# The Pool mixing of a two-layer decoder step in three rounded passes, with a ring of six weight places

## The chip, the cores and the metric

The kernel runs on one core of a Trainium2 chip. It is written for the engines by hand: TensorE (PE, with its weight loads as PEld), VectorE (DVE), ScalarE (ACT), GpSimd (POOL) and SyncE (SP), which issues the DMAs. The metric is the device time of one execution in microseconds (us), the median of several runs.

## What is computed

The reference is one inference step of a decoder with two layers, for a prompt of 1024 tokens and 32 sample tokens (8 x 4), together T = 1056 columns. Layer 0 mixes tokens by multi-scale pooling:

```
zp = rms_norm(x) @ w_in_pool        # u (1536) | gate (1536) | memory query (512) | memory gate (512)
for g, w in enumerate((2, 4, 8, 16)):                     # four groups of 384 channels
    means = trailing mean of u over w positions
pooled = means - u
mixed = einsum('btgc,gcd->btgd', pooled, w_grp)           # 384 x 384 for each group
branch = mixed * scale
y = [branch * silu(gate), memory_attention * silu(memory gate)] @ w_out
x = x + y
```

Layer 1 does stick-breaking attention in the place of the pooling; the change doesn't touch it. Everything is float32.

## The kernel before

**Stages.** The layers come one after the other. Layer 0 is `front_phase` (norms, keys and values of the memory tokens, the transposed tokens; up to 91 us), `pool_phase` (the projection, the pooling, the mixing; 91 to 512 us), `memory_attention_phase` (to 597 us) and `out_phase`. Between two phases stands a barrier of all engines.

**The projection.** `Quads` computes the projection in pairs of 128-column blocks, 16 pairs p in layer 0, each by Strassen's scheme in seven products, P1 to P7 (`self.seq` has their order: P5, P4 of the pair before, P1, P2, P6, P3, P7). A product is 24 matmuls on 264 columns, since each float32 product is made in three rounded passes: high weights by high tokens (L320), high weights by low tokens (L321), low weights by high tokens (L322). "fp32r" is the rounded kind of float32. GpSimd combines the weights (`combine`, L192 to L204), ScalarE rounds them (`round`, L226) and VectorE subtracts for the remainder (`remainder`, L233). The weights stand in a ring of `RING` = 8 places, and each engine prepares the weights `AHEAD` = 7 products ahead of the one in hand. ScalarE copies P1, P6, P4 and P5 out of their banks (`copy`), VectorE adds P2, P3 and P7 (`add`). In the first products the tokens too have to be split, by ScalarE (`token_high`, L274) and VectorE (`token_rest`, L279).

**The groups.** Pairs 0 to 3 give queries and memory gates; then each group of the pooling has three pairs (`first(n) = 4 + 3 * n` is its first): u, u; u, gate; gate, gate. Its pooling (`pool_part`, VectorE) is spread over the products behind, and its mixing (`group`) comes behind product P1 of the next group's first pair, for the last group behind the last product. `group` transposes the kept rows for the state outputs (L1278) and makes nine outputs, three row blocks m by three column parts u, each of three float32 matmuls on 352 columns (L1291; the trace has two records for each such matmul, 54 in all). The outputs alternate between two banks, and VectorE scales and gates each (L1234). When y is out, SyncE stores it (L1064, in three parts), and then loads the next group's state (L1050) and mixing weights (L1052). TensorE turns that state (`turn_state`, L1270) behind product P2 of the next group's first pair:

```
                for i, (p, x) in enumerate(q.seq):
                    q.product(pe, i)
                    for n in range(GROUPS):
                        if n and (p, x) == (first(n), "P1"):
                            group(n - 1)
                        if (p, x) == (first(n), "P2"):
                            turn_state(n)
                group(GROUPS - 1)
```

**The end of the stage.** SyncE loads the first three pages of the samples' memory keys into freed memory (L931), and behind the last product of the projection the queries (`memory.queries`, L938), their scales (L939) and the prompt's own keys (L935); then it finishes the last group. GpSimd pads the samples' queries (`memory.pad`, L943, L950). The next stage's SyncE first waits until the last group's stores have landed (`memory.tail`) and then loads pages 3 and 4 of the keys (a_more, L931), which TensorE turns (L1526) behind pages 0 to 2.

**The end of the front.** `front_phase` prepares the first six weights of the ring beside its own work. GpSimd's combination for P3 (L204) waits for the remainder of P2's weights, the third of the ring; GpSimd's three token sums of tile 6 (L248, L254, L256) stand behind it, and VectorE's `other_sums(7)` (L248 on) waits for those.

Of the kernel before, what the change touches and what calls it, by code (L numbers as in the profile page):

```python
# [88 lines left out]
RING, AHEAD = 8, 7  # L89


class Quads:
# [11 lines left out]
    def __init__(self, nc, k, c, i, src, columns):  # L104
        self.nc, self.k, self.i, self.src, self.columns, self.n = nc, k, i, src, columns, len(columns)
        self.full, self.lo = [], []
        for n in range(7):
            self.allocate_tokens(n)
        self.w_hi = k.sb("w_hi", [P, RING, K2, P], F32R)
        self.w_full, self.w_lo = self.two_kinds("w_lo", [P, RING, K2, P])  # L110
# [46 lines left out]

    def load_b(self, sp, p):
# [23 lines left out]
    def combine(self, gp, i):  # L182
# [5 lines left out]
        if x == "P5":  # L188
            if i >= RING:
                gp.wait_ge(self.done, 2 * (i - RING) + 2)  # L190
            gp.wait_ge(self.loaded_b[p % 2], 16 * (p // 2 + 1))
            gp.tensor_tensor(self.w_full[:, i % RING, :, :], a21, a22, ALU.add).then_inc(self.combined, 1)  # L192
# [13 lines left out]
    def source(self, i):  # L206
        p, x = self.seq[i]
        if x == "P5":
            return self.w_full[:, i % RING, :, :]
# [3 lines left out]
    def round(self, act, i):  # L213
# [4 lines left out]
        if i >= RING:  # L218
            act.wait_ge(self.done, 2 * (i - RING) + 2)
# [6 lines left out]
        act.activation(self.w_hi[:, i % RING, :, :], self.source(i), ACT.Copy).then_inc(self.high, 1)  # L226

    def remainder(self, dve, i):
# [4 lines left out]
        dve.tensor_tensor(self.w_lo[:, i % RING, :, :], self.source(i), self.w_hi[:, i % RING, :, :].bitcast(F32),  # L233
# [64 lines left out]
    def product(self, pe, i):  # L298
# [4 lines left out]
        for n in range(2):  # L303
# [13 lines left out]
            for kk in range(K2):  # L317
                w_hi, w_lo = self.w_hi[:, i % RING, kk, :], self.w_lo[:, i % RING, kk, :]
# [108 lines left out]
def front_phase(nc, c, A, O, S, q, source):  # L427

    with ExitStack() as ctx:
# [35 lines left out]
        with nc.Block() as block:  # L465
# [71 lines left out]
            def _(act):  # L537
# [123 lines left out]
                for j in range(3):  # L661
# [12 lines left out]
            def _(dve):  # L674
# [134 lines left out]
                for j in range(3):  # L809
# [3 lines left out]
                first_sum(7)  # L813
                other_sums(7)
# [85 lines left out]
class MemoryAhead:  # L900
# [11 lines left out]
    def __init__(self, nc, k, c, A, S, i):  # L912
        self.nc, self.c, self.A, self.S, self.i = nc, c, A, S, i
        self.at = nc.sbuf_top - self.BELOW[i] - self.SIZE
        self.kl = [k.sem(f"kl{n}") for n in range(self.PAGES[i])]
# [21 lines left out]
    def queries(self, sp):  # L937
        sp.dma_start(self.qT[:, :, :], self.S[f"mq{self.i}"].rearrange("h p t -> p h t")).then_inc(self.ql, 16)  # L938
        sp.dma_start(self.rs[:, :], self.S[f"rs{self.i}"]).then_inc(self.rl, 16)  # L939

    def pad(self, gp):
# [3 lines left out]
        gp.wait_ge(self.ql, 16)  # L945
# [63 lines left out]
def pool_phase(nc, c, A, O, S, q, memory):  # L1009

    with ExitStack() as ctx:
# [6 lines left out]
        wg = k.sb("wg", [P, GB, GW])  # L1018
        up = k.sb("up", [P, GB, HIST + T])
        us = k.sb("us", [P, GB, NB_S, SX])  # L1020
        sums = [k.sb(f"sum{i}", [P, EXT]) for i in range(2)]
# [7 lines left out]
        tail = k.sb("tail", [KEPT, GW])  # L1029
        q.allocate_banks(k)  # L1030
        aux = k.ps("aux", 2)
        names = "gated zeroed keeps stl sturned wgl mready mixed pooled sums tailt tailc stored ystored carried".split()
# [9 lines left out]
        with nc.Block() as block:  # L1042
            @block.sync
            def _(sp):
# [9 lines left out]
                def finish_group(n):  # L1054
# [3 lines left out]
                    sp.dma_start(O["pool_p"][0, 0, :, g * GW:(g + 1) * GW], tail[0:HIST, :]  # L1058
                                 ).then_inc(memory.tail if last else s["stored"], 16)
                    sp.dma_start(O["pool_s"][0, :, HIST - T_S:HIST, g * GW:(g + 1) * GW], tail[HIST:KEPT, :]  # L1060
                                 ).then_inc(memory.tail if last else s["stored"], 16)
# [4 lines left out]
                for j in range(AHEAD - 1):  # L1066
# [3 lines left out]
                for i, (p, x) in enumerate(q.seq):  # L1070
                    q.loads(sp, i + AHEAD - 1)
# [21 lines left out]
                memory.queries(sp)  # L1093
# [9 lines left out]
            def _(gp):  # L1103
# [11 lines left out]
                for j in range(6, AHEAD + 1):  # L1115
                    q.combine(gp, j)
                for i, (p, x) in enumerate(q.seq):
                    q.combine(gp, i + AHEAD + 1)
# [16 lines left out]
            def _(act):  # L1135
                def begin(p):
# [13 lines left out]
                    q.copy(act, p, "P5", part(p, 1, 1), ACT.Copy)  # L1150
                q.tokens_scalar(act, 0)
                for j in range(6, AHEAD):
                    q.round(act, j)
                for i, (p, x) in enumerate(q.seq):
                    q.round(act, i + AHEAD)
# [1979 lines left out]
```

## Time and profile before

| | us |
|---|---|
| median of 3 runs | 2334.16 |
| lowest and highest | 2331.37, 2334.32 |
| profiled execution | 2338.4 |
| its span in the trace | 2336.7 |
| TensorE busy | 2201.2 |
| VectorE busy | 1292.6 |
| ScalarE busy | 1009.2 |
| GpSimd busy | 433.0 |

Times in the trace count from the span's start. A busy time is the union of an engine's instructions, and matmuls are pipelined, so that a busy TensorE is not one at its peak; the distance from one start to the next is what a matmul takes of a run. An idle time in square brackets is what the engine stood before an instruction, with what ended it.

### The profile page before, as it was taken

What the parts mean: (1) busy time and instruction counts of PE and PEld (TensorE: products, weight loads), DVE (VectorE), ACT (ScalarE), POOL (GpSimd) and SP (SyncE); (2) the same over time, 40 slices, a digit from 0 to 9 for tenths busy, and PEclk for the clock granted to TensorE, in tenths of its full rate; (3) what the DMA queues carried; (4) which work ended last, traced back from release to release, by engine and by line L of the source; (5) the groups of instructions that cost most, each with busy time, mean ns of one, the idle gap of its engine ahead of it and who ended that gap; (6) DMA issues with size and microseconds to landing.
All of it is one profiled execution on the core that took longest, in us unless ns stands there. A gap on an engine that the chain in (4) does not pass through costs nothing. (4 is left out here: it accounts for less than half of the span.)

```text
span 2336.7 us, 47103 instructions
## 1 busy us (share of the span) xinstructions
PE 2201.2 (94%) x18709; PEld 1834.6 (79%) x18709; DVE 1292.6 (55%) x2040; ACT 1009.2 (43%) x2090; POOL 433.0 (19%) x542
## 2 busy tenths in 40 slices
PE   7799999997999689999999998889999999998999
PEld 6799899886688589999999997766666566654787
DVE  6846666435422374334444443588888888875211
ACT  7533223215311144333333343457777777775100
POOL 0533223202000043222222221321121111100000
PEclk9899999998899889999999999889999999999999
DMA  8222222144635553334433336789999999978331
GB/s 289 86 87 89 79 64 66 66 166 163 210 119 155 146 186 102 109 99 133 153 106 109 96 96 234 253 292 379 396 407 393 406 395 388 375 284 307 123 108 55
DMA packets 283274, 453.98 MB, mean 194 GB/s; under 512 B 30962, under 2 KB 208062, under 8 KB 283038
## 3 DMA queue, kind: packets, MB, share of 16 engines
q1 hardware_dynamic: 274958, 421.83, 51.8%
q0 software_dynamic: 8000, 29.10, 3.3%
q8 instruction: 149, 2.44, 0.4%
q14 instruction: 71, 0.58, 0.1%
q10 hardware_dynamic: 96, 0.02, 0.0%
HBM read 372.43 MB, written 78.43 MB: 193 GB/s over the span
## 5 line engine op out<-in xcount | busy, mean ns | idle before, releaser
L233 DVE TENSOR_TENSOR h_w_lo<-l_w,h_w_hi 128x512 fp32r<-128x512 f32 x264 | 213.7, 811 | 221.2 <-ACT h_w_hi L226 218.7
L226 ACT ACTIVATE h_w_hi<-l_w 128x512 fp32r<-128x512 f32 x264 | 166.7, 633 | 239.9 <-PE i_c L322 81.4
L320 PE MATMUL i_x<-h_t_hi,h_w_hi 128*128 128x264 f32 x560 | 163.3, 292 | 6.8 <-DVE h_t_lo L279 6.8
L2960 PEld LDWEIGHTS b_krow<-ar_arena,b_qd 128*32 128x32 f32 x3072 | 107.2, 111 | 72.6 <-issue 57.0
L192 POOL TENSOR_TENSOR h_w_lo_full<-l_w 128x512 f32<-128x512 f32 x44 | 57.5, 1308 | 560.5 <-DMA l_w<-in_w_in_sb_dram 229.9
L320 PE MATMUL i_y<-h_t_hi,h_w_hi 128*128 128x264 f32 x560 | 161.3, 288 | 0.0
L322 PE MATMUL i_x<-h_t_hi,h_w_lo 128*128 128x264 f32 x560 | 161.0, 287 | 0.0
L321 PE MATMUL i_x<-h_t_lo,h_w_hi 128*128 128x264 f32 x560 | 160.4, 286 | 0.0
L321 PE MATMUL i_y<-h_t_lo,h_w_hi 128*128 128x264 f32 x560 | 159.0, 284 | 0.0
L322 PE MATMUL i_y<-h_t_hi,h_w_lo 128*128 128x264 f32 x560 | 158.9, 284 | 0.0
L2960 PE MATMUL b_krow<-ar_arena,b_qd 128*32 128x128 f32 x3072 | 140.7, 279 | 7.9 <-ACT b_kev L2666 6.9
L320 PE MATMUL i_c<-h_t_hi,h_w_hi 128*128 128x264 f32 x448 | 129.4, 289 | 17.8 <-DVE h_t_lo L279 17.4
L2789 DVE STREAM_TRANSPOSE ar_arena<-ar_arena 128x768 f32<-128x768 f32 x146 | 140.7, 967 | 1.3 <-PE b_krow L2960 1.3
L2907 PE MATMUL b_zbank<-bf_qh,bf_kh 128*128 128x512 f32 (+3 forms) x288 | 133.7, 548 | 2.2 <-PEq L76 2.2
L321 PE MATMUL i_c<-h_t_lo,h_w_hi 128*128 128x264 f32 x448 | 128.4, 287 | 0.0
L322 PE MATMUL i_c<-h_t_hi,h_w_lo 128*128 128x264 f32 x448 | 128.1, 286 | 0.0
L2647 ACT ACTIVATE b_a<-b_a 128x512 f32<-128x512 f32 (+2 forms) x144 | 75.2, 522 | 104.1 <-DVE b_a L2749 103.4
L2923 PE MATMUL b_obank<-b_a,b_vh 128*128 128x512 f32 (+3 forms) x288 | 117.9, 491 | 1.8 <-issue 0.8
L200 POOL TENSOR_TENSOR l_w<-l_w 128x512 f32<-128x512 f32 x44 | 65.3, 1485 | 282.1 <-DVE h_w_lo L233 282.1
L320 PEld LDWEIGHTS i_x<-h_t_hi,h_w_hi 128*128 128x128 f32 x560 | 107.0, 191 | 7.5 <-issue 7.4
L321 PEld LDWEIGHTS i_x<-h_t_lo,h_w_hi 128*128 128x128 f32 x560 | 107.2, 192 | 0.0
L322 PEld LDWEIGHTS i_x<-h_t_hi,h_w_lo 128*128 128x128 f32 x560 | 107.1, 191 | 0.0
(368 smaller groups left out, 6424.9 us busy)
## 6 DMA issues: line engine op xcount, KB each, us to landing
ar_arena<-in_cache_sb_k_dram SPq DMA_DIRECT2D x73, 768.0 KB, 9.7
bf_vpage<-in_cache_sb_v_dram SPq DMA_DIRECT2D x64, 768.0 KB, 8.8
b_vpage<-in_cache_sb_v_dram SPq DMA_DIRECT2D x64, 768.0 KB, 8.5
l_w<-in_w_in_sb_dram SPq DMA_DIRECT2D x56, 512.0 KB, 3.9
l_w<-in_cache_sb_k_dram SPq DMA_DIRECT2D x36, 768.0 KB, 9.4
l_w<-in_w_in_pool_dram SPq DMA_DIRECT2D x32, 512.0 KB, 4.2
bf_kpage<-in_cache_sb_k_dram SPq DMA_DIRECT2D x19, 768.0 KB
ar_arena<-scratch_yT SPq DMA_DIRECT2D x14, 1024.0 KB, 6.6
```

The source lines that it names most:

```text
L192: gp.tensor_tensor(self.w_full[:, i % RING, :, :], a21, a22, ALU.add).then_inc(self.combined, 1)
L200: gp.tensor_tensor(a11, a22, a21, ALU.subtract).then_inc(self.combined, 1)
L226: act.activation(self.w_hi[:, i % RING, :, :], self.source(i), ACT.Copy).then_inc(self.high, 1)
L233: dve.tensor_tensor(self.w_lo[:, i % RING, :, :], self.source(i), self.w_hi[:, i % RING, :, :].bitcast(F32), ALU.subtract).then_inc(self.r ...
L320: pe.matmul(out, w_hi, t_hi, start=kk == 0 and x in ("P1", "P2", "P5"), stop=False, skip_group_check=True)
L321: pe.matmul(out, w_hi, t_lo, start=False, stop=False, skip_group_check=True)
L322: ins = pe.matmul(out, w_lo, t_hi, start=False, stop=kk == K2 - 1, skip_group_check=True)
L2647: act.activation(a[:, t % 3, 0:n], a[:, t % 3, 0:n], ACT.Exp).then_inc(s["ax"], 1)
L2789: dve.transpose(kt[u % 2][:, :, :, x * Q:(x + 1) * Q].rearrange("p h f j -> p (h f) j"), kpage[n % NK][:, u % 2 * HH * HD:(u % 2 + 1) * HH ...
L2907: ins = pe.matmul(zbank[t % 2][:, 0:n], kh[:, h % 2, kb * P:(kb + 1) * P], qh[:, h % 2, q0:q0 + n], start=True, stop=not diag, skip_group_ ...
L2923: pe.matmul(obank[:, 512 - n:512], vh[:, h % 2, kb, :], a[:, t % 3, 0:n], start=first, stop=last, skip_group_check=True).then_inc(s["pvd"], 1)
L2960: ins = pe.matmul(krow[pair * CT:(pair + 1) * CT, 0:P], qd[:, i % 2, at:at + CT], kt[u % 2][:, h, f, :], start=odd == 0 and f == 0, stop=o ...
```

## The change

It does five things. (1) The mixing is computed in three rounded passes (`product3`) on split pooled rows (`up_hi` in the two pooling buffers, `up_lo` over `up`) and split weights (`wg_hi`, `wg_lo` over `wg`). ScalarE rounds the weights in `mix_weights` and the rows in `mix_high`, in three parts of 128 x 1056 elements over two buffers; VectorE subtracts in `mix_weights` and `mix_low`. (2) The outputs come column part by column part, so that all three stores of y wait for the last three outputs. (3) The mixing of a group comes behind P2 of the next pair instead of P1. (4) In layer 0 the ring has six places (`self.ring`) and a lead of five (`self.ahead`); the two places that come free hold `wg_hi` and the tail rows. In the front, weights 2 and 3 are rounded later and remainder 2 stands behind `first_sum(7)`. (5) Head 0 of the queries and the prompt's own keys are loaded behind the last output of the last mixing (`mready`), since their place is in use until then; heads 1 to 3 behind the last product as before.

```diff
@@ Quads.__init__
+        self.ring = PLACES if i else PLACES - 2
+        self.ahead = self.ring - 1
...
@@ front_phase, scalar
                 act.wait_ge(s["made"], 12)
-                for j in range(3):
+                for j in range(2):
                     q.round(act, j)
                 key_root(1)
                 evacuate(7)
-                q.round(act, 3)
                 act.wait_ge(s["made"], 14)
-                for j in range(4, 6):
+                for j in range(2, 6):
                     q.round(act, j)
@@ front_phase, vector
-                for j in range(3):
+                for j in range(2):
                     q.remainder(dve, j)
                 key_normed(1)
                 evacuate(7)
                 first_sum(7)
+                q.remainder(dve, 2)
                 other_sums(7)
@@ pool_phase, sync
                     for m in range(GB):
-                        sp.wait_ge(s["mixed"], 9 * n + 3 * m + 3)
+                        sp.wait_ge(s["mixed"], 9 * n + 7 + m)
                         sp.dma_start(S["yT0"][g * GB + m], gate[:, m, :])
...
                 sp.wait_ge(q.done, 2 * len(q.seq))
-                memory.queries(sp)
+                memory.queries(sp, 1, MH)
+                memory.scales(sp)
+                sp.wait_ge(s["mready"], 9 * GROUPS)
+                memory.queries(sp, 0, 1)
                 memory.own_keys(sp)
                 finish_group(GROUPS - 1)
@@ pool_phase, scalar
+                def mix_weights(n):
+                    act.wait_ge(s["wgl"], 16 * (n + 1))
+                    if n:
+                        act.wait_ge(s["mready"], 9 * n)
+                    for kk in range(GB):
+                        act.activation(wg_hi[kk], wg[:, kk, :], ACT.Copy).then_inc(s["wgh"], 1)
+
+                def mix_high(n):
+                    act.wait_ge(s["pooled"], GB * (n + 1))
+                    for u in range(NT):
+                        if u >= 2:
+                            act.wait_ge(s["mready"], 9 * n + 3 * (u - 1))
+                        act.activation(up_hi[u % 2], up[:, :, HIST + u * TT:HIST + (u + 1) * TT], ACT.Copy
+                                       ).then_inc(s["uph"], 1)
...
+                        for n in range(1, GROUPS):
+                            if p + 1 == first(n):
+                                mix_high(n - 1)
                         if p + 1 < q.n:
                             begin(p + 1)
...
+                mix_high(GROUPS - 1)
@@ pool_phase, vector
+                def mix_low(n, u):
+                    dve.wait_ge(s["uph"], NT * n + u + 1)
+                    cols = slice(HIST + u * TT, HIST + (u + 1) * TT)
+                    dve.tensor_tensor(up_lo[:, :, cols], up[:, :, cols], up_hi[u % 2].bitcast(F32), ALU.subtract
+                                      ).then_inc(s["upr"], 1)
+
                 def mix(n):
+                    mix_low(n, 0)
+                    mix_low(n, 1)
...
+                    for u in range(NT):
+                        if u == 1:
+                            mix_low(n, 2)
+                        for m in range(GB):
+                            dve.wait_ge(s["mready"], 9 * n + 3 * u + m + 1)
@@ pool_phase, tensor
-                    pe.wait_ge(s["wgl"], 16 * (n + 1))
-                    for m in range(GB):
-                        for u in range(NT):
-                            at = 3 * m + u
+                    pe.wait_ge(s["wgr"], GB * (n + 1))
+                    for u in range(NT):
+                        pe.wait_ge(s["upr"], NT * n + u + 1)
+                        for m in range(GB):
+                            at = 3 * u + m
...
-                        if n and (p, x) == (first(n), "P1"):
+                        if n and (p, x) == (first(n), "P2"):
                             group(n - 1)
                         if (p, x) == (first(n), "P2"):
                             turn_state(n)
```

TensorE, at the first group's mixing, before: behind the last pass of P1 (bank y) come the transposes of the kept rows, the 27 float32 matmuls, P2 (bank x, of its 24 passes the first and last are shown), and the turning of the state.

```order
L322 MATMUL p_y<-h_t_hi,h_w_lo 128x264
L1278 MATMUL p_aux<-c_ident,p_kept 47x128 x3
L1291 MATMUL p_aux<-p_up,p_wg 128x352 x27
L320 MATMUL p_x<-h_t_hi,h_w_hi 128x264
...
L322 MATMUL p_x<-h_t_hi,h_w_lo 128x264
L1270 MATMUL p_aux<-c_ident,p_state 128x120 x3
L320 MATMUL p_y<-h_t_hi,h_w_hi 128x264
```

The same place after the change; the nine passes of an output read the rounded rows (p_sum_r, p_up_r) and weights (h_w_hi, h_w_lo, p_wg_r), and 81 stand between the transposes and the turning.

```order
L328 MATMUL p_x<-h_t_hi,h_w_lo 128x264
L1340 MATMUL p_aux<-c_ident,p_kept 47x128 x3
L81 MATMUL p_aux<-p_sum_r,h_w_hi 128x352
L82 MATMUL p_aux<-p_up_r,h_w_hi 128x352
L83 MATMUL p_aux<-p_sum_r,p_wg_r 128x352
...
L83 MATMUL p_aux<-p_sum_r,p_wg_r 128x352
L1332 MATMUL p_aux<-c_ident,p_state 128x120 x3
L326 MATMUL p_y<-h_t_hi,h_w_hi 128x264
```

P2 (bank x) has moved from between the mixing and the turning to ahead of both; P6 (bank y) follows the turning as before.

SyncE at the end of the Pool stage, before: queries of four heads, scales, own keys, then the tails and the stores of y.

```order
L938 DMA mp_qT<-scratch_mq 128x4x1056
L939 DMA mp_rs<-scratch_rs 128x33
L935 DMA mp_own<-scratch_mkT 128x1024
L1058 DMA out_pool_p_dram<-p_tail 15x384
L1060 DMA out_pool_s_dram<-p_tail 8x4x384
L1064 DMA scratch_yT<-p_gate 128x1056 x3
```

And after the change, where the wait for the last output stands ahead of the second load of queries:

```order
L945 DMA mp_qT<-scratch_mq 128x3x1056
L949 DMA mp_rs<-scratch_rs 128x33
L945 DMA mp_qT<-scratch_mq 128x1056
L942 DMA mp_own<-scratch_mkT 128x1024
L1075 DMA out_pool_p_dram<-h_w_lo_full 15x384
L1077 DMA out_pool_s_dram<-h_w_lo_full 8x4x384
L1081 DMA scratch_yT<-p_gate 128x1056 x3
```

One load of queries has become two, and all but the first two rows now come behind that wait; the tail rows are read from the ring's spare place.

## Rows read from the trace of the kernel before

**Rows 1.** The page's first part: busy time, share of the span, instructions.
```profile
PE 2201.2 (94%) x18709; PEld 1834.6 (79%) x18709; DVE 1292.6 (55%) x2040; ACT 1009.2 (43%) x2090; POOL 433.0 (19%) x542
```
**Rows 2.** Stretches: length, busy PE, PEld, DVE, ACT, POOL; PE clock, DMA share, GB/s.
```profile
100.00:110.00 10.00, 9.95 (x82) 9.74 (x80) 10.00 (x10) 7.71 (x11) 4.57 (x2) 1.00 0.18 52
210.00:240.00 30.00, 30.00 (x249) 30.00 (x248) 26.67 (x39) 11.87 (x26) 11.62 (x11) 1.00 0.19 54
273.00:280.00 7.00, 4.85 (x40) 4.64 (x39) 5.26 (x7) 2.91 (x7) 2.54 (x2) 1.00 0.57 188
355.00:365.00 10.00, 7.34 (x49) 7.13 (x48) 4.48 (x7) 2.56 (x6) 2.54 (x2) 0.83 0.39 123
436.00:446.00 10.00, 8.08 (x55) 7.88 (x54) 4.82 (x7) 3.50 (x9) 2.55 (x2) 0.83 0.41 132
511.00:597.00 86.00, 65.67 (x435) 54.57 (x434) 41.21 (x83) 34.42 (x91) 15.89 (x16) 0.84 0.51 182
```
**Rows 3.** Timeline of TensorE at the first mixing: start, duration, instruction, idle before.
```profile
256.97 16.15 PE L1291 MATMUL p_aux<-p_up,p_wg 128*128 128x352 f32 x54
272.69 0.55 PE L320 MATMUL p_x<-h_t_hi,h_w_hi 128*128 128x264 f32 x1
...
278.18 0.53 PE L1270 MATMUL p_aux<-c_ident,p_state 120*128 120x120 f32 x3 [2.15 <-DMA p_state<-in_state_pool_dram]
```
**Rows 4.** Waits of TensorE, 85 to 600 us: in total, times, longest.
```profile
PE p_aux L1270 <- DMA p_state<-in_state_pool_dram: 6.7, 3, 2.7
...
PE a_bank L1526 <- DMA a_more<-in_cache_mem_k_dram: 0.4, 1, 0.4
```
**Rows 5.** Timeline of TensorE: rounded passes of 264 and of 512 columns.
```profile
253.00 0.29 PE L320 MATMUL p_x<-h_t_hi,h_w_hi 128*128 128x264 f32 x1
253.12 0.28 PE L321 MATMUL p_x<-h_t_lo,h_w_hi 128*128 128x264 f32 x1
...
633.72 0.39 PE L81 MATMUL o_bank<-ar_w_hi,o_y_hi 128*128 128x512 f32 x1
633.95 0.39 PE L82 MATMUL o_bank<-ar_w_lo,o_y_hi 128*128 128x512 f32 x1
```
**Rows 6.** Timeline of SyncE: behind the first mixing, and around the stage's end.
```profile
274.22 0.37 SPq L1050 DMA_DIRECT2D p_state<-in_state_pool_dram  x1
...
494.94 0.37 SPq L938 DMA_DIRECT2D mp_qT<-scratch_mq  x1
...
501.15 10.98 SPq L1064 DMA_DIRECT2D scratch_yT<-p_gate  x3
514.46 0.90 SPq L931 DMA_DIRECT2D a_more<-in_cache_mem_k_dram  x2
```
**Rows 7.** DMA issues, 240 to 300 and 495 to 530: KB, us to landing.
```profile
scratch_yT<-p_gate SPq DMA_DIRECT2D x3, 528.0 KB, 3.0
p_state<-in_state_pool_dram SPq DMA_DIRECT2D x1, 180.0 KB, 3.9
...
mp_qT<-scratch_mq SPq DMA_DIRECT2D x1, 2112.0 KB, 7.8
```
**Rows 8.** Timeline of ScalarE behind the last product.
```profile
495.17 1.07 ACT L1170 ACTIVATE p_gate<-p_gate 128x1056 f32<-128x1056 f32 x1
496.15 0.63 ACT L1171 ACTIVATE p_gate<-p_gate 128x528 f32<-128x528 f32 x1
```
**Rows 9.** Timelines of GpSimd, VectorE and TensorE: the front's end, the stage's start.
```profile
79.20 1.27 POOL L204 TENSOR_TENSOR l_w<-l_w 128x512 f32<-128x512 f32 x1
...
84.71 0.69 DVE L248 TENSOR_TENSOR h_t_lo_full<-h_t_lo_full 128x512 f32<-128x512 f32 x1 [2.45 <-POOL h_t_lo_full L256]
...
89.55 0.28 DVE L256 TENSOR_TENSOR h_t_lo_full<-h_t_lo_full 128x128 f32<-128x128 f32 x1
91.95 2.50 DVE L279 TENSOR_TENSOR h_t_lo<-h_t_lo_full,h_t_hi 128x1056 fp32r<-128x1056 f32 x2 [2.12 <-ACT h_t_hi L274]
...
112.31 0.36 PE L320 MATMUL p_x<-h_t_hi,h_w_hi 128*128 128x264 f32 x1 [2.14 <-issue]
```

More of the change, by code:

```diff
@@ L88 @@
 K2 = KD // 2
-RING, AHEAD = 8, 7
+PLACES = 8
 class Quads:
@@ L935, in own_keys, with queries, scales @@
         sp.dma_start(self.own[:, :, :].rearrange("p h m -> p (h m)"), self.S["mkT"][self.i]).then_inc(self.ol, 16)
-    def queries(self, sp):
-        sp.dma_start(self.qT[:, :, :], self.S[f"mq{self.i}"].rearrange("h p t -> p h t")).then_inc(self.ql, 16)
+    def queries(self, sp, first=0, last=MH):
+        sp.dma_start(self.qT[:, first:last, :], self.S[f"mq{self.i}"][first:last].rearrange("h p t -> p h t")
+                     ).then_inc(self.ql, 16)
+    def scales(self, sp):
         sp.dma_start(self.rs[:, :], self.S[f"rs{self.i}"]).then_inc(self.rl, 16)
@@ L1017, in pool_phase, with two_kinds @@
         first = lambda n: 4 + 3 * n
-        wg = k.sb("wg", [P, GB, GW])
-        up = k.sb("up", [P, GB, HIST + T])
+        def two_kinds(name, shape):
+            full = k.sb(name, shape)
+            size = 4 * shape[1] * (shape[2] if len(shape) == 3 else 1)
+            return full, nc.alloc_sbuf_tensor_at(f"p_{name}_r", shape, F32R, offset=nc.sbuf_base - size)
+        wg, wg_lo = two_kinds("wg", [P, GB, GW])
+        up, up_lo = two_kinds("up", [P, GB, HIST + T])
         us = k.sb("us", [P, GB, NB_S, SX])
-        sums = [k.sb(f"sum{i}", [P, EXT]) for i in range(2)]
+        sums, up_hi = zip(*(two_kinds(f"sum{i}", [P, GB * TT]) for i in range(2)))
+        up_hi = [a[:, :].rearrange("p (k t) -> p k t", k=GB) for a in up_hi]
+        spare = lambda ring: ring[:, 0:PLACES - q.ring, :, :].rearrange("p r k n -> p (r k n)")
+        wg_hi = [spare(q.w_hi)[:, 0:GW], spare(q.w_hi)[:, GW:2 * GW], spare(q.w_lo)[:, 0:GW]]
         ssum = [k.sb(f"ssum{i}", [P, NB_S, SX]) for i in range(2)]
@@ L1070, in _ @@
                 for i, (p, x) in enumerate(q.seq):
-                    q.loads(sp, i + AHEAD - 1)
+                    q.loads(sp, i + q.ahead - 1)
                     if x == "P4" and p < 4:
@@ L1238, in _ @@
                 q.tokens_vector(dve, 0)
-                for j in range(6, AHEAD):
+                for j in range(6, q.ahead):
                     q.remainder(dve, j)
@@ L1244, in _ @@
                             mix(n - 1)
-                    q.remainder(dve, i + AHEAD)
+                    if i + q.ahead >= 6:
+                        q.remainder(dve, i + q.ahead)
                     if x == "P2":
@@ L1542, in scores @@
                     else:
-                        pe.wait_ge(memory.ql, 16)
+                        pe.wait_ge(memory.ql, 16 * memory.parts)
                         pe.wait_ge(memory.ol, 16)
@@ L2105, in _ @@
                     q.token_fetch(sp, S["tok"], t)
-                for j in range(AHEAD - 1):
+                for j in range(q.ahead - 1):
                     q.loads(sp, j)
                 for i, (p, x) in enumerate(q.seq):
-                    q.loads(sp, i + AHEAD - 1)
+                    q.loads(sp, i + q.ahead - 1)
                     kind, h = kinds[p]
@@ L2133, in _ @@
                         memory.queries(sp)
+                        memory.scales(sp)
                     if (p, x) == (q.n - 1, "P3"):
@@ L2142, in _ @@
             def _(gp):
-                for j in range(AHEAD + 1):
+                for j in range(q.ahead + 1):
                     q.combine(gp, j)
                 for i, (p, x) in enumerate(q.seq):
-                    q.combine(gp, i + AHEAD + 1)
+                    q.combine(gp, i + q.ahead + 1)
                     if (p, x) in ((0, "P4"), (1, "P4")):
```

70 lines of the change are left out of this document (41 added, 29 removed).

## The prediction

> **What bounds the kernel now.** The page comes first [rows 1]: TensorE is busy 2201.2 of 2336.7 us. What the change is worth is so to be read on TensorE's own sequence in the Pool stage (91 to 512 us): how much shorter the mixing gets, and where TensorE newly waits. The timeline of TensorE [rows 3] shows the pattern at a mixing: 54 half-matmuls in one run of 16.15 us, product P2 from 272.69, a wait of 2.15 us for the next group's state, the turning of it at 278.18. The waits [rows 4] say that this is nearly all that stops it: 6.7 us in three waits for p_state. The table of stretches [rows 2] shows the holes behind the mixings (273 to 280, 355 to 365, 436 to 446) and the stage behind (511 to 597), where TensorE is busy only 65.67 of 86 us. VectorE is filled in two places: at the stage's start (10.00 of 10 us) and ahead of the first mixing (26.67 of 30).
>
> **The mixing itself.** Nine outputs take 16.15 us less the last pass's tail of some 0.15, 1.78 us each [rows 3]. The new output is nine rounded passes of 352 columns. No such pass is in the trace, but it has two neighbours [rows 5]: passes of 264 columns start 0.121 us apart (253.00, 253.12) and passes of 512 columns 0.23 (633.72, 633.95). Both are some 0.457 ns a column, so 352 take 0.161 us and an output 9 x 0.161 = 1.45 us. Saved: 36 x (1.78 - 1.45) = **-11.8 us**. Bounds: at 0.147 us a pass (352 columns at 2.4 GHz) it would be -16; at 0.17, -9.
>
> **Waits in the mixing.** The third piece of the rounded rows waits for the third output. ScalarE then needs 1.07 us (its Silu of 128x1056 [rows 8]) and VectorE 1.25 (2.50 for two pieces of 128x1056 [rows 9]); with an eviction and signals behind them it is 3.1 us, while TensorE has two outputs (2.9 us) to go. I take 0.3 us of waiting a group, and once more 0.3 in the first, where three weight remainders come ahead of the pooling's end: **+1.5 us** (0 to 5).
>
> **The cover that goes.** The state's load is issued 1.5 us behind the last output (274.22 [rows 6] against 272.69 [rows 3]) and has landed at 278.18: 5.5 us, of which P2 hid its own 24 x 0.121 = 2.9 us. Now P2 runs ahead of the mixing, where it hides the rounding on ScalarE and VectorE, and the turning stands directly behind the mixing. The load is still issued only when the last output is out, so TensorE waits 5.5 us and each of three groups pays 2.9 us: **+8.8 us** (8 to 9; the order leaves it no other cover). ScalarE's copies of P5 and P1, which P6 needs, end some 2.5 us behind the mixing, and so lie under this wait, as do the weights: P6, P3 and P7 are rounded before ScalarE and VectorE enter the mixing. Besides, the stores of y used to be issued over 10.98 us for three [rows 6], and will now go 1.45 us apart, directly ahead of the state; one lands in 3.0 us, the state in 3.9 [rows 7]. Some of a store is still moving when the state starts: 0.3 us each, **+0.9 us** (0 to 4).
>
> **The clock.** Over the 10 us around the second and the third wait the granted clock is 0.83, around the first 1.00 [rows 2]. So two of the three waits cost a spell at 1.2 GHz of (1 - 0.83) x 10 / 0.5 = 3.4 us, in which half the work is lost, 1.7 us. With waits of 5.5 us I expect all three to cost it, and one more at the last mixing: four spells for two, **+3.4 us** (-3 to +8). The Trainium skill ("TensorE: Matmul & The Clock Gate", "Part 1: The HAM clock gate") states that the clock has two levels and that an idle array falls back to the lower one until it has been busy again. By that rule all four waits pay, as I took it; by the trace's two in three it would be 2.3 us less.
>
> **The last mixing.** No P2 stands ahead of it, and its rounding stands behind the last Silus. SyncE's first issue at 494.94 [rows 6] marks the end of the last product, and the mixing began there. ScalarE's chain ends at 496.15 + 0.63 = 496.8 [rows 8]; then 1.07 for rounding and 1.25 for the remainder, with 0.1 of signals: 499.2. With the three transposes (0.3) taken off the wait: **+4.1 us** (2.5 to 6).
>
> **The seam to the memory stage.** Before, SyncE issued queries, scales, own keys and small tails from 494.94 on, beside the mixing; behind the last output only one store of y, whose issue ends at 501.15 + 10.98 = 512.1. An eviction, an issue of 0.3 and signals lie between, so the last output was out at about 511.15. The next stage's first page of keys waits until all stores have landed, is issued at 514.46 [rows 6], and TensorE stands 0.4 us for it [rows 4]: this wait ends last there. Now head 0 of the queries (528 KB), own keys (512 KB), two tails (70 KB) and three y (1584 KB) all come behind the last output, 2694 KB. In rows 7, 528 KB take 3.0 us and 2112 KB 7.8 us, so 330 KB/us past the first: 3.0 + 2166/330 = 9.6 us. The page goes out 9.6 us behind the last output instead of 3.3: **+6.2 us** (2.5, SyncE's extra issues alone, to 8). The Trainium skill ("DMA: Bandwidth & Descriptors", "Anatomy of one DMA") gives 2.0 us plus bytes / 436e3 for a transfer; by it these 2.76 MB take 8.3 us and this term is 5.0.
>
> **Start of the stage.** The third remainder now stands behind first_sum(7) in the front. GpSimd's combination for P3 (79.20) waits for it, GpSimd's three sums stand behind that, and VectorE waited 2.45 us for those sums until 84.71 and ended the front at 89.8 [rows 9]. With the remainder done near 81.6 instead of 79, all of it comes 2.5 us later: **+2.5 us** (0 to 2.5). In return two remainders of some 0.7 us and the far-ahead roundings no longer stand between the token parts, where VectorE is full [rows 2], and P7's wait of 2.14 us at 112.31 [rows 9] and one behind it go: **-2.5 us** (-3 to 0).
>
> **Sum** against the profiled execution (2338.4 us): -11.8 + 1.5 + 8.8 + 0.9 + 3.4 + 4.1 + 6.2 + 2.5 - 2.5 = **+13.1**, so 2351.5. The median of the runs shown, 2334.16, is 4.2 lower; there it is **2347.3 us**, 0.56% slower. A measurement of this kernel can tell some 0.2%, 4.7 us, from no change.
>
> **Rivals.**
> - *The seam is hidden.* If the memory stage's tiles do not wait for the samples' keys, 5 of the seam's 6.2 us vanish in its idle time [rows 2]: +8, 2342. Against it: TensorE's order is fixed and the page stood in its way [rows 4]. 0.17.
> - *The next stage swallows everything (not slower).* It has 20 us of idle time on TensorE. If its end is set by transfers that do not start with the stage, the seam, the last mixing and its spell (6.2 + 4.1 + 1.7 = 12.0) vanish: +1, 2335. This decides only if some load there goes out at a fixed time; for it speaks the idle time alone, against it that all its loads stand in SyncE's queue behind the pages. 0.10.
> - *The waits keep the clock.* If none costs a spell the clock term is -3.4 and the sum +6, 2340: 0.08. Faster by over 0.2% needs the seam hidden too (-6.2), the start's gain without its loss (-2.5) and the cheaper bound of the mixing (-4): -7, 2327: 0.03.
> - *VectorE becomes the bound.* Ahead of the first mixing it is full [rows 2]; it gets three weight remainders and three row remainders (1.25 us each) a group, with a lead of five products instead of seven. If TensorE then waits for its additions, 1.5 to 2 us a group: +20, 2354. Against it: after the first group fewer additions are pooled. 0.14.
> - That the mixing remains in float32 is excluded by the instructions: nine an output, on rounded operands as in rows 5.
>
> **How the numbers follow.** The forecast's case (+9 to +17) has 0.48. The range takes in the kept clock and VectorE's case and leaves out the swallowing and the faster one: 2338 to 2355. Slower by over 0.2%: 0.48 + 0.17 + 0.14 + most of 0.08 = 0.86; within: 0.11; faster: 0.03.
>
> **What would show it.** Evictions 1.45 us apart; behind three mixings a wait of 5 to 6 us for p_state; 4 us of idle time ahead of the last mixing; the first page of keys issued 9 to 10 us behind the last output; the front ending 2.5 us later, and P7 not waiting. I am wrong if evictions lie over 1.6 us apart, if p_state lands within 3 us of the mixing's end, or if the seam is as long as before.

## The result, and the profile after

The changed kernel takes 2350.06 us (median of 20 runs) against 2333.38 of the kernel before: ratio 1.0070, 95% interval [1.0057, 1.0084], so +13 to +20 us. It is slower by 0.7%; 0.56% was forecast, at 2347.3. One of the 20 runs took 3328 us at a granted clock of 0.60 and is left out of the ratio and its interval. The profiled execution took 2352.5 us (span 2350.8) against 2338.4 (2336.7).

The page's first part answers to [rows 1]:

```profile
PE 2195.3 (93%) x18817; PEld 1847.7 (79%) x18817; DVE 1296.1 (55%) x2064; ACT 1025.5 (44%) x2114; POOL 432.0 (18%) x542
```

TensorE is busy 5.9 us less and the kernel is 14.1 us longer: what was saved in work came back as waits. The timeline of TensorE at the first mixing, then that of VectorE, which empties its banks, then that of SyncE [rows 3, 6]:

```profile
256.70 0.49 PE L1340 MATMUL p_aux<-c_ident,p_kept 128*47 128x128 f32 x3
256.94 0.41 PE L81 MATMUL p_aux<-p_sum_r,h_w_hi 128*128 128x352 f32 x1
...
270.24 0.32 PE L83 MATMUL p_aux<-p_sum_r,p_wg_r 128*128 128x352 f32 x1
276.08 0.86 PE L1332 MATMUL p_aux<-c_ident,p_state 120*128 120x120 f32 x3 [5.51 <-DMA p_state<-in_state_pool_dram]
```
```profile
262.70 1.26 DVE L1276 TENSOR_TENSOR p_up_r<-p_up,p_sum_r 128x1056 fp32r<-128x1056 f32 x1 [0.54 <-ACT p_sum_r L1184]
263.87 1.18 DVE L1293 SCALAR_TENSOR_TENSOR p_gate<-p_aux,c_vec,p_gate 128x352 f32<-128x352 f32 x2
266.26 0.58 DVE L1293 SCALAR_TENSOR_TENSOR p_gate<-p_aux,c_vec,p_gate 128x352 f32<-128x352 f32 x1 [1.20 <-PE p_aux L83]
267.71 0.58 DVE L1293 SCALAR_TENSOR_TENSOR p_gate<-p_aux,c_vec,p_gate 128x352 f32<-128x352 f32 x1 [0.87 <-PE p_aux L83]
```
```profile
268.32 3.21 SPq L1081 DMA_DIRECT2D scratch_yT<-p_gate  x3
272.07 0.37 SPq L1067 DMA_DIRECT2D p_state<-in_state_pool_dram  x1
```

The evictions lie 1.45 us apart, not 1.78: the mixing itself became as short as forecast. The third remainder, made at 262.70, holds two evictions up until 263.87, but in all the nine outputs take 13.5 us, 0.4 more than 9 x 1.45. Behind them TensorE has nothing to do for 5.51 us, where it waited 2.15 [rows 3]. The waits of TensorE, 85 to 620 us [rows 4]:

```profile
PE p_aux L1332 <- DMA p_state<-in_state_pool_dram: 15.0, 3, 5.5
...
PE a_bank L1590 <- PEq L76: 6.3, 1, 6.3
...
PE p_aux L81 <- issue: 4.0, 1, 4.0
...
PE a_bank L1590 <- DMA a_more<-in_cache_mem_k_dram: 1.0, 1, 1.0
```

The 6.7 us for p_state have become 15.0; the 4.0 us are ahead of the last mixing. Its beginning, on ScalarE, VectorE and TensorE:

```profile
495.52 2.05 ACT L1184 ACTIVATE p_sum_r<-p_up 128x1056 fp32r<-128x1056 f32 x2
```
```profile
496.62 2.43 DVE L1276 TENSOR_TENSOR p_up_r<-p_up,p_sum_r 128x1056 fp32r<-128x1056 f32 x2 [5.37 <-ACT p_sum_r L1184]
```
```profile
493.53 0.49 PE L1340 MATMUL p_aux<-c_ident,p_kept 128*47 128x128 f32 x3
497.99 0.63 PE L81 MATMUL p_aux<-p_sum_r,h_w_hi 128*128 128x352 f32 x1 [3.97 <-issue]
...
499.00 0.49 PE L81 MATMUL p_aux<-p_sum_r,h_w_hi 128*128 128x352 f32 x1
499.30 0.49 PE L82 MATMUL p_aux<-p_up_r,h_w_hi 128*128 128x352 f32 x1
```

Rounding waits behind the last Silus on ScalarE, the remainders behind the rounding, and TensorE behind both. The first passes then start 0.29 us apart instead of 0.16, the lower of the clock's two levels (352 columns at 1.2 GHz), so that from its first pass to its last this mixing takes 14.6 us where the other three take 13.3. The seam to the memory stage, SyncE's timeline [rows 6]:

```profile
512.93 0.33 SPq L945 DMA_DIRECT2D mp_qT<-scratch_mq  x1
513.31 0.43 SPq L942 DMA_DIRECT2D mp_own<-scratch_mkT  x1
...
514.98 2.15 SPq L1081 DMA_DIRECT2D scratch_yT<-p_gate  x3
522.10 0.91 SPq L938 DMA_DIRECT2D a_more<-in_cache_mem_k_dram  x2
```

The first page of keys goes out at 522.10, 9.2 us behind the last output at 512.9; before it was 3.3. The stretches behind the mixings, around the last one's beginning, and the memory stage [rows 2] (length, busy PE, clock, DMA share, GB/s):

```profile
271.00:281.00 10.00, 4.92 (x30) 0.83 0.69 221
353.00:363.00 10.00, 5.33 (x32) 0.83 0.72 234
434.00:444.00 10.00, 5.41 (x31) 0.83 0.77 260
493.00:503.00 10.00, 6.03 (x32) 0.83 0.48 164
...
511.00:605.00 94.00, 70.89 (x446) 0.82 0.53 190
```

All three waits now have a granted clock of 0.83 around them, where one had 1.00, and so has the start of the last mixing, where the kernel before has 1.00 in the same 10 us. In the out phase (L2094), which began at 598.00 and begins at 606.19, the kernel is 8.2 us late; by the end it is 14.1. The other 5.9 us arise in code that the change does not touch.

### The profile page after: what moved, and what is told of

Its sections match the earlier page's. It is cut to its first block and busy times, and to the rows that moved or that the text cites. A ratio compares the mean times of both kernels' runs of the same rounds, so it can differ in the third digit from the quotient of the medians.

```text
span 2350.8 us, 47383 instructions
## 1 busy us (share of the span) xinstructions
PE 2195.3 (93%) x18817; PEld 1847.7 (79%) x18817; DVE 1296.1 (55%) x2064; ACT 1025.5 (44%) x2114; POOL 432.0 (18%) x542
## 5 line engine op out<-in xcount | busy, mean ns | idle before, releaser
L239 DVE TENSOR_TENSOR h_w_lo<-l_w,h_w_hi 128x512 fp32r<-128x512 f32 x264 | 204.1, 774 | 221.6 <-ACT h_w_hi L232 220.0
```

The lines of the kernel that those rows point to most:

```text
L239: dve.tensor_tensor(self.w_lo[:, self.slot(i), :, :], self.source(i), self.w_hi[:, self.slot(i), :, :].bitcast(F32), ALU.subtract).then_in ...
```

## Experiments

Each was timed beside the kernel before on the same chip: 1 to 4 on one, 5, 6, 7 and 9 on a second, 8 and 10 to 12 on a third. The bold number is the ratio and its interval, less one, times 2333 us: what it takes against the kernel before. The changed kernel stands at **+16.3 (13 to 20)** by the same reckoning. Single profiles are read by stretches, since their start and their clock differ by several us.

**1. The position alone.** In the kernel before:

```
-                        if n and (p, x) == (first(n), "P1"):
+                        if n and (p, x) == (first(n), "P2"):
                             group(n - 1)
```

> The kernel before, with one line changed: a mixing stands behind P2 of the next pair instead of behind P1. Theory (the cover that goes): the state's load is no longer hidden by P2, so three waits for p_state grow from 2.2 us to about 5.1 each, +8.8 us, with up to +3 for the clock, and the last mixing is untouched: +8 to +12 us against the kernel before. Rival (the waits are filled in any case, since P6 behind the turning waits for ScalarE's copies of P5 and P1): under +4 us.

2348.24 us, ratio 1.0080 [1.0058, 1.0102]: **+19 (14 to 24)**. Its waits:

```profile
PE p_aux L1270 <- DMA p_state<-in_state_pool_dram: 14.0, 3, 5.1
```

One line costs as much as the whole change. The theory named its place; its size is above the 12 us expected. The wait grew from 6.7 to 14.0 us, 7.3. Around the three waits the clock was

```profile
271.00:281.00 10.00, 5.51 (x22) 0.78 0.44 148
355.00:365.00 10.00, 5.53 (x22) 0.84 0.51 177
440.00:450.00 10.00, 4.92 (x19) 0.86 0.51 178
```

and from the second turning of the state to the third 85.6 us passed, against 81.5 in the profile of before and 79.6 in that of experiment 3, where the code up to the last mixing is the kernel before's. Against that profile this one is 16.3 us later from the stage's first product to the last eviction: 9.3 us of it are the longer waits (14.0 against 4.8), and 7.1 the clock: the last of the 24 passes behind each turning starts 2.2 to 2.5 us later than there.

**2. The ring of six alone.** The changed kernel with float32 mixing, its old place and the old end of the stage.

```
-RING, AHEAD = 8, 7
+PLACES = 8
...
+        self.ring = PLACES if i else PLACES - 2
+        self.ahead = self.ring - 1
```

> The changed kernel with the mixing in float32, its place behind P1 and the end of the stage as in the kernel before; the ring of six places, the lead of five and the new order in the front stay. Theory: the shorter lead costs nothing, P7's wait of 2.1 us at the start goes and the front's extra wait of 2.7 us comes: -2 to +2 us against the kernel before, its p_state waits as before (6.7 us in all). Rival (VectorE or the ring becomes the bound, with waits of TensorE for w_hi, w_lo or the additions): +5 us or more.

2338.09 us, 1.0022 [1.0005, 1.0039]: **+5 (1 to 9)**. The waits do not show where: p_state stands at

```profile
PE p_aux L1284 <- DMA p_state<-in_state_pool_dram: 6.8, 3, 2.6
```

and P7's wait of 2.1 us is gone, as expected; no wait for w_hi, w_lo or an addition is new. The rival's sign in the time is half there, its mechanism is not. In this profile the extra time does not lie in the Pool stage: the out phase begins at 592.58, earlier than in the kernel before (598.00), and from there to the end, in code that is the same in both, it takes 1744.8 us against 1738.7. I leave this as 0 to 5 us, unexplained.

**3. The seam alone.** In the kernel before:

```
-                memory.queries(sp)
+                memory.queries(sp, 1, MH)
+                memory.scales(sp)
+                sp.wait_ge(s["mready"], 9 * GROUPS)
+                memory.queries(sp, 0, 1)
                 memory.own_keys(sp)
                 finish_group(GROUPS - 1)
```

> The kernel before, with only the end of the Pool stage of the changed one: three heads of the queries and the scales at the last product, head 0, own keys, tails and y behind the last output. Theory (the seam): the first page goes out about 9 us behind the last output instead of 3.3, +6 us (4 to 8) on the time. Rival (the memory stage's own idle time takes it up): under +2 us.

2338.32 us, 1.0042 [1.0022, 1.0062]: **+10 (5 to 14)**. SyncE's timeline, with the last eviction at 503.79:

```profile
503.78 0.33 SPq L939 DMA_DIRECT2D mp_qT<-scratch_mq  x1
...
505.83 2.54 SPq L1068 DMA_DIRECT2D scratch_yT<-p_gate  x3
513.05 0.90 SPq L932 DMA_DIRECT2D a_more<-in_cache_mem_k_dram  x2
```

The page goes out 9.3 us behind it, and the out phase begins 93.4 us behind it, where the profile of before has 86.8: +6.6 us, none of it taken up by the memory stage's idle time. Up to its last mixing this kernel is the one before, and serves as a second look at it:

```profile
PE p_aux L1277 <- DMA p_state<-in_state_pool_dram: 4.8, 3, 1.6
```

With waits of at most 1.6 us the clock stayed at 1.00 behind all three mixings, and the third turning came at 434.46 instead of 440.36. Two profiles of the same code thus differ by 6 us up to there, and the one that the forecast was read from is the later.

**4. The state's load early.** In the changed kernel SyncE issues it a pair and a half ahead; it needs only the earlier turning of its place, not the mixing:

```
                 def load_group(n):
                     if n:
-                        sp.wait_ge(s["sturned"], n)
                         sp.wait_ge(s["mready"], 9 * n)
-                    sp.dma_start(state[:, :], ...
...
                     for n in range(1, GROUPS):
+                        if (p, x) == (first(n) - 1, "P1"):
+                            load_state(n)
```

> The changed kernel, with the load of the pooling state issued a pair and a half ahead, as soon as the place has been turned, instead of behind the last output of the mixing; the weights' load stays behind it. Theory: the three waits of 5 us for p_state go; what remains is the last eviction or ScalarE's copies, 1.5 to 2.5 us each, and with them clock spells go: -9 to -15 us against the changed kernel, so +2 to +8 against the kernel before. Rival (the copies and the clock's recovery take the same time): less than 4 us of gain.

2336.42 us, 1.0019 [1.0002, 1.0036]: **+4 (0 to 8)**, 12 below the changed kernel. Its waits, the second turning, and the stretches behind the mixings:

```profile
PE p_aux L1339 <- DVE p_gate L1300: 2.3, 3, 0.8
```
```profile
352.28 0.50 PE L1339 MATMUL p_aux<-c_ident,p_state 120*128 120x120 f32 x3 [0.77 <-DVE p_gate L1300]
353.16 0.36 PE L326 MATMUL p_x<-h_t_hi,h_w_hi 128*128 128x264 f32 x1 [0.39 <-ACT p_up L335]
```
```profile
270.00:280.00 10.00, 8.85 (x63) 1.00 0.64 229
348.00:358.00 10.00, 8.85 (x65) 1.00 0.77 267
425.00:435.00 10.00, 8.85 (x65) 1.00 0.79 271
```

Of each 5 us, 0.8 is left for the last eviction and 0.4 for ScalarE's copies, and the clock stays up. From turning to turning it is 76.8 us instead of 81.5.

**5. The turning later, the load as late as in the changed kernel.** On TensorE, with VectorE's use of the turned state (`history`) moved to P3 in the same way:

```
-                        if (p, x) == (first(n), "P2"):
+                        if (p, x) == (first(n), "P3" if n else "P2"):
                             turn_state(n)
```

> The changed kernel, with the turning of the state (groups 1 to 3) behind P3 instead of directly behind the mixing, and VectorE's use of it moved with it; the load is issued as late as now. Theory (the cover that went is the cost): P6 and P3 hide 5.8 us of the load's 5.5, the three waits of 5 us go and only a wait for ScalarE's copies in P6 of up to 1 us stays: -9 to -14 us against the changed kernel, like the early load. Rival (the wait for p_state hid another of the same length, for the copies or additions that P6 needs): the wait reappears at P6 and the gain is under 4 us.

2335.35 us, 1.0011 [0.9997, 1.0025]: **+3 (-1 to +6)**, 14 below the changed kernel. The wait for p_state is gone; what is left is P6's wait for the copies, at its longest

```profile
351.07 0.36 PE L326 MATMUL p_x<-h_t_hi,h_w_hi 128*128 128x264 f32 x1 [1.65 <-ACT p_up L335]
```

So the copies that P6 needs are late by 1.65 us at most, not by 5: the wait for the state had hidden them. Products between a mixing and the turning are the cover; experiments 1, 4 and 5 take it away, make it needless, and give it back, and agree.

**6. The last rounding early.** ScalarE rounds the last group's first two pieces at P2 and P3 of the last pair, VectorE makes their remainders at P3 and P7:

```
+                    if (p, x) in ((q.n - 1, "P2"), (q.n - 1, "P3")):
+                        mix_high(GROUPS - 1, (("P2", "P3").index(x),))
...
+                    if (p, x) in ((q.n - 1, "P3"), (q.n - 1, "P7")):
+                        mix_low(GROUPS - 1, ("P3", "P7").index(x))
```

> The changed kernel, with the first two row pieces of the last group rounded by ScalarE at P2 and P3 of the last pair and their remainders made by VectorE at P3 and P7, instead of behind the last product. Theory: TensorE's 4.0 us ahead of the last mixing shrink to under 1, -3 to -5 us against the changed kernel. Rival (VectorE or ScalarE has no room in the last pair, so P7 or P4 waits instead): 0 to +2.

2349.40 us, 1.0060 [1.0039, 1.0081]: **+14 (9 to 19)**, not told apart from the changed kernel. The stretch itself did what was expected; TensorE's and VectorE's timelines:

```profile
499.08 0.49 PE L1345 MATMUL p_aux<-c_ident,p_kept 128*47 128x128 f32 x3
```
```profile
501.21 0.58 DVE L1296 SCALAR_TENSOR_TENSOR p_gate<-p_aux,c_vec,p_gate 128x352 f32<-128x352 f32 x1 [1.05 <-ACT p_gate L1207]
...
513.07 0.58 DVE L1296 SCALAR_TENSOR_TENSOR p_gate<-p_aux,c_vec,p_gate 128x352 f32<-128x352 f32 x1 [0.87 <-PE p_aux L83]
```

From the transposes to the last eviction 14.0 us instead of 19.4 (493.53 to 512.94), and no wait ahead of the mixing. But this execution reached the first turning 3.8 us later, in unchanged code.

**7. Another end of the stage.** The rounded group weights and the tail change places, so that no head of the queries waits for the mixing; y is stored by thirds of its columns; own keys go last:

```
-                    for m in range(GB):
-                        sp.wait_ge(s["mixed"], 9 * n + 7 + m)
-                        sp.dma_start(S["yT0"][g * GB + m], gate[:, m, :])...
+                    for u in range(NT):
+                        sp.wait_ge(s["mixed"], 9 * n + 3 * u + 3)
+                        sp.dma_start(S["yT0"][g * GB:(g + 1) * GB, :, unit(u)].rearrange("m p t -> p m t"),
+                                     gate[:, :, unit(u)])...
```

> The changed kernel with another end of the stage: the rounded group weights and the saved tail exchange their places, so that all four heads of the queries go out at the last product; y goes out by thirds of its columns as the mixing makes them, and own keys last. Behind the last output stand 528 KB of y and 512 KB of own keys, which the pages do not wait for. Theory (the bytes behind the last output set the seam): the first page goes out 3 to 4 us behind the last output instead of 9.2, -5 to -6 us against the changed kernel, and the state, no longer behind three bunched stores, comes up to 1 us sooner in each group. Rival (the memory stage's idle time takes it up, or the thirds cost more in short rows): under 2 us.

2348.57 us, 1.0071 [1.0050, 1.0091]: **+17 (12 to 21)**. Again no difference in the median, and again the stretch is shorter. SyncE at the seam and behind the first mixing:

```profile
518.94 0.49 SPq L942 DMA_DIRECT2D mp_own<-scratch_mkT  x1
521.75 0.90 SPq L938 DMA_DIRECT2D a_more<-in_cache_mem_k_dram  x2
```
```profile
274.40 0.37 SPq L1067 DMA_DIRECT2D p_state<-in_state_pool_dram  x1
```

The last eviction is at 517.92, so the page goes out 3.8 us behind it and the out phase 86.4, not 93.25. The state lands 4.0 us behind its issue (turned at 278.40), exactly as with bunched stores (272.07 to 276.08): that part of the theory fell.

**8. Six and seven together**, the state still late.

> The changed kernel with the last group's rounding early and the other end of the stage, but the state's load as late as in the changed kernel. Alone, these two moved the median by less than the 5 us that such a comparison can tell, though their own stretches of the trace got 4.9 and 6.8 us shorter. Theory (the two costs are real and what hid them was chance in the clock): together -8 to -12 us against the changed kernel, so +5 to +9 against the kernel before. Rival (they are worth something only where the state comes early): -4 us or less.

2336.03 us, 1.0017 [1.0001, 1.0033]: **+4 (0 to 8)**. Against the changed kernel on the same chip (experiment 12) it is 12 us less by the medians and 9 by the ratios. The two stretches give 5.4 + 6.8 = 12.2 together, although either alone showed nothing. Six runs resolve about 5 us here; that both fell short by chance is the simplest reading, but only their sum is shown.

**9. All three corrections.**

> The changed kernel with all three: the state's load early, the last group's rounding early, the other end of the stage. If the three costs are separate, as the prediction's sum has them, it saves 12 + 4 + 6 = 22 us against the changed kernel: 2328, 5 us below the kernel before. Rival (one hides the other, for example the last mixing starts earlier but the stores end no sooner): 2333 to 2338.

2321.87 us, 0.9949 [0.9929, 0.9969]: **-12 (-17 to -7)**, faster than both kernels. It lies 28 us below the changed kernel; 22 were expected. Against experiment 4, which has the early load alone, it is 16 us, where the two stretches give 12.2. The page of keys goes out at 500.70 with the last eviction at 496.90.

**10. The early load in the kernel before.**

> The kernel before (float32 mixing behind P1, ring of eight), with only the state's load issued early. Theory: three waits of 1.6 to 2.7 us for p_state shrink to the wait for the last eviction, which P2 hides, -5 to -7 us, and up to -3 for the clock: 2323 to 2328. If so, half of the lead of the kernel with all three corrections is not the rounded passes' but the state's. Rival (a wait for ScalarE's copies takes its place): above 2330.

2326.63 us, 0.9970 [0.9956, 0.9984]: **-7 (-10 to -4)**. By the medians, more than half of what experiment 9 gains was there to be had without the change. Between its turnings 77.8 us pass, between those of experiment 9 76.8: the rounded passes are worth about 1 us a group against a fairly set float32 kernel, for behind P2 they pay the 1.2 us for eviction and copies that P2 covered. In time the two differ by 5 us, with intervals that overlap.

**11. Both cures of the state.**

> The kernel with all three corrections, with the turning of the state moved behind P3 besides. What is left at the turning is 0.8 us a group for the last eviction: theory -1 to -3 us against that kernel (2319 to 2321); rival (the pooling starts later on VectorE and waits appear ahead of the next mixing): 0 to +3.

2324.43 us, 0.9958 [0.9942, 0.9974]: **-10 (-14 to -6)**. Not told apart from experiment 9: no gain is shown.

**12. The changed kernel once more.**

> The changed kernel once more, beside the others on the same chip. Of the 14.1 us between the two profiled executions, 5.9 arose behind the start of the out phase, in code that the change does not touch. Theory (chance in the clock spells): this profile's stretch from the start of the out phase to the end lies anywhere between 1734 and 1745 us, as in the other runs, and the median stays at 2347 to 2352. Rival (the later start of the stages itself costs 6 us behind them): it is 1744 or more again.

2348.39 us, 1.0057 [1.0035, 1.0079]: the slowdown repeats. From the start of the out phase to the end 1744.2 us passed, again as in the first profile (1744.6), which is what the rival said. The other profiles have 1738.7 (before), 1738.9, 1740.7, 1742.1 and 1744.8 with float32 mixing, and 1736.1 to 1745.2 with rounded passes. The float32 kernel of experiment 2 reached 1744.8 as well, with an early start (592.58), so lateness alone is not the cause; and the waits alone are not either: the three profiles with both the late state and the late seam (with experiment 6's 1745.2) lie at the upper end, but experiments 7 and 8, with the same waits for the state, have 1739.2 and 1737.9, and 4 and 5, with the same seam, 1740.7 and 1736.1. What those 4 to 6 us are stays open.

## Why the prediction was right, and where it was not

| step | predicted | shown |
|---|---|---|
| mixing itself | -11.8 | evictions 1.45 us apart: -0.33 x 36 = -11.8 |
| waits in the mixing | +1.5 | the first three take 13.3 us from first pass to last, 0.4 over 80 x 0.161: about +1.6 for four |
| cover that goes | +8.8 | p_state 15.0 us against 6.7: +8.3 (4.8 in experiment 3: +10.2); 5.5, 4.9 and 4.6 each, where 5 to 6 was named |
| y bunched ahead of the state | +0.9 | 0: 4.0 us to land in either order |
| clock | +3.4 | four spells instead of two: +2.7, in experiment 12 +4.3 (below) |
| last mixing | +4.1 | wait of 3.97; 5.4 us gone in experiment 6, the wait and its 1.3 of clock |
| seam | +6.2 | page 9.2 us behind the last output, not 3.3: +5.9; experiment 3 +6.6 |
| start of the stage | 0 | front +1.8, from there to P7 -1.6 (below); the ring's experiment +5 (1 to 9) |

**The cover was the step that decided**, and its price is told twice over: put into the kernel before it cost 19 us, taken out of the changed one in two different ways it gave back 12 and 14. The forecast's cover, stores and clock together were 13.1 for it.

**The clock** can be read from the passes themselves. From the turning of the state to the last of the 24 passes of the product behind it, 3.17 us go by where the granted clock is 1.00 (all three times in experiment 3). In the changed kernel the passes behind the first turning start 0.22 us apart at first, the lower of the two levels, and 0.12 later:

```profile
277.19 0.42 PE L328 MATMUL p_y<-h_t_hi,h_w_lo 128*128 128x264 f32 x1
277.41 0.42 PE L326 MATMUL p_y<-h_t_hi,h_w_hi 128*128 128x264 f32 x1
```

The same stretch takes 4.5, 4.7 and 4.7 us there, 4.3 us more in sum, and the last mixing another 1.3: 5.6. In the kernel before it is 3.2, 4.7 and 4.6, 3.0 more in sum. That makes +2.7 for the forecast's +3.4; experiment 12, with 5.1 three times and 1.4 in the last mixing, makes +4.3. So the price of a spell (1.7 forecast; 1.3 to 2.0 in these profiles, up to 2.5 in experiment 1) was right, and so was the fourth spell at the last mixing. The count of two in the kernel before was luck: I took it from a single profile, and the second look at the same code (experiment 3) had none, against which the change costs 5.6 us of clock. From turning to turning the changed kernel takes 81.5 to 82.0 us in its two profiles, experiment 4 76.8.

**The seam** was right against its rival: the memory stage has 20 us of idle time on TensorE, and none took up the 6 us. That this is because all of its loads stand behind the pages fits, but was not tried by itself. The row "PEq, 6.3 us" above names a second thing that I had not put into the chain: key turning starts only when GpSimd has padded the queries (516.65 to 517.79; the turning starts at 519.22, behind the barrier), and head 0 of them comes behind the last output too. That the page is still waited for behind it (1.0 us) says that the page is the later of the two; what the padding would cost alone was not tried. By the figure of the Trainium skill ("DMA: Bandwidth & Descriptors", "Anatomy of one DMA"), which that section gives for one transfer on GpSimd's path, the same bytes would take an estimated 8.3 us. Here several transfers went out from SyncE's queue; the 9.2 from output to issue, with the issues in between, lie nearer to the row-based 9.6, but the two differ by little over one microsecond.

**The start** was forecast as +2.5 for the front and -2.5 behind it. In the profile VectorE's wait in the front grew from 2.45 to 5.17 us and P7's fell from 2.14 to 0.36:

```profile
84.89 0.69 DVE L254 TENSOR_TENSOR h_t_lo_full<-h_t_lo_full 128x512 f32<-128x512 f32 x1 [5.17 <-POOL h_t_lo_full L262]
```
```profile
110.85 0.36 PE L326 MATMUL p_x<-h_t_hi,h_w_hi 128*128 128x264 f32 x1 [0.36 <-issue]
```

Over all profiles the stage's first product lies at 91.97 to 93.44 with the old front (four) and at 92.50 to 96.03 with the new one (ten), on average 1.6 us later. Read by stretches, both parts are there and both smaller than forecast. From VectorE's copy of the last full tile of tokens to the first product it is 13.5 us in the four profiles with the old front and 15.9 in this one and those of experiments 2 and 12; that is 2.4, less the 0.6 of the remainder that no longer stands ahead of the copy: +1.8. From the first product to P7 it is 17.3 us instead of 18.9: -1.6.

**The sum** was +13.1 against a measured +16.3 (13 to 20). The cases forecast as the rivals did not come: VectorE did not become the bound, the seam was not hidden, none of the long waits kept its clock. The forecast lies at the interval's lower edge. What the working may lack is the 4 to 6 us of the untouched later stages (experiment 12) and the ring's (experiment 2); neither has an explanation here. The five terms that the three corrections answer to, 8.8 + 0.9 + 3.4 + 4.1 + 6.2 = 23.4 us, gave 28 in experiment 9, and the four that stay, -11.8 + 1.5 + 2.5 - 2.5 = -10.3, compare with its -12 (-17 to -7) against the kernel before. One reading was wrong: that the waits for p_state are nearly all that stops TensorE [rows 4] holds only from the first mixing to the last. In the whole stretch of that view, 85 to 600 us, there are also 9.8 us ahead of the stage's first product (13.7 with the new front) and more in the memory stage.

## What to carry to other kernels

When work is moved to make room for a preparation, ask what the old position was covering: here one product behind the mixing hid half of a load, and moving it cost more than the faster arithmetic gave. A transfer that waits for a whole group of conditions should be split by what each part needs; the state's load never needed the mixing, and issuing it early is worth 7 us to the old kernel and 12 to the new one. And a gain or a loss of a few us in one stretch must be looked for in that stretch: the median of six runs hid 5 and 7 us that were plain in the timeline.

## What the hardware showed that was not expected

The same idle time lowers the granted clock by a different amount in two executions of the same kernel, and that number says little of the time lost. Around the same waits of 4.5 to 5.5 us the first profile of the changed kernel had 0.83 in all three stretches; its second, on the same stretches, had

```profile
271.00:281.00 10.00, 4.48 (x22) 0.66 0.75 247
353.00:363.00 10.00, 5.49 (x28) 0.66 0.84 282
434.00:444.00 10.00, 5.38 (x29) 0.71 0.87 294
```

yet from turning to turning it took only 0.3 and 0.5 us more (81.9 and 82.0 against 81.6 and 81.5): part of the low clock lay in idle time. Whether the execution or the chip makes the difference is open, since it is not known that both ran on one chip. Waits of at most 1.6 us (experiment 3) or 0.8 (experiment 4) left it at 1.00 every time, and those of 1.8 to 2.7 us in the kernel before and experiment 2 lowered it behind three mixings of six, behind one of 1.9 but not behind one of 2.5. Waits of over 4 us behind a mixing lowered it in all six profiles that have them, which agrees with the rule of the Trainium skill ("TensorE: Matmul & The Clock Gate", "Part 1: The HAM clock gate") that an idle array loses its clock; how long it stays low afterwards was not to be had from one profile.
